# Attention that steps over pairs of heads instead of single heads

## What is computed

```
M1 (mixer of the first block):
  4 memory heads:  p = softmax(q k^T / 8)                       256 queries x 256 memory keys
  6 forgetting heads: p = softmax(q k^T / 8 + c_query - c_key)  causal, c = cumsum(log_f)
  6 gated groups:  out = gelu(u) * (tril(w_s) @ rmsnorm(gelu(v)) + b_s)
MA (sliding window, 16 heads, 2 key/value heads):
  s = q k^T / 8 + bias[t5_bucket(distance)];  window of 128;  softmax with a sink
MB (latent attention, 16 heads, 96-wide q and k):
  s = q k^T / sqrt(96), causal;  q, k normed, 32 of the 96 columns rotated
each: o = p @ v, then o @ w_out added to x
```

## Time and profile before

| | |
|---|---|
| Median of 3 runs | 1393.72 us (1381.62 to 1393.95) |
| Span of the profiled execution | 1392.3 us |
| PE busy | 1329.8 us, 96% of the span, 8874 matmuls |
| DVE busy | 749.8 us, 54% |
| ACT busy | 609.7 us, 44% |
| POOL busy | 116.0 us, 8% |
| Chain that ended last | PE 68% of the span; L244 to L246 20% each, L467 3%, L492 2%, L480 1% |
| Mean granted clock of PE | 0.953 |

### The profile page before, as it was taken

The page is one execution under the profiler, slowest core; times in us unless marked ns, Lnnn a source line. Parts: engine busy times, 40 slices in busy tenths (PEclk is TensorE's granted clock), DMA queues, the critical chain, the costliest instruction groups (busy, mean ns, idle before and its releaser), DMA issues.

```text
span 1392.3 us, 21334 instructions
## 1 busy us (share of the span) xinstructions
PE 1329.8 (96%) x8874; PEld 1200.9 (86%) x8874; DVE 749.8 (54%) x932; ACT 609.7 (44%) x790; POOL 116.0 (8%) x163
## 2 busy tenths in 40 slices
PE   6989989999899999989999999999999889999998
PEld 6885789999799999875889999899999768999997
DVE  4784355555465555564365555555554585555554
ACT  5463244444443344454343344443333586444432
POOL 3440010000210000031000000100000160000000
PEclk9996799999999999985899999999999989999999
DMA  9961035556465555451145555465555402455530
GB/s 312 334 184 42 31 120 184 181 185 209 135 216 182 181 184 192 140 171 35 61 152 182 182 188 191 132 208 190 184 181 172 135 31 65 149 184 191 193 127 31
DMA packets 167091, 220.87 MB, mean 159 GB/s; under 512 B 6014, under 2 KB 148412, under 8 KB 166892
## 3 DMA queue, kind: packets, MB, share of 16 engines
q1 hardware_dynamic: 164572, 212.28, 47.2%
q0 software_dynamic: 2448, 7.58, 1.7%
HBM read 212.47 MB, written 7.37 MB: 158 GB/s over the span
## 4 chain that ended last, share of the span: by engine, by line
PE 68%; DVE 2%; ACT 1%; issue 1%; POOL 0%; POOLq 0%; DVEq 0%; ACTq 0%
PE ps L244 20%; PE ps L245 20%; PE ps L246 20%; PE ps L467 3%; PE ps L492 2%; PE ps L480 1%; PE ps L344 1%; PE ps L493 1%; DVE x L387 1%; ACT w_hi L218 0%; DVE h_lo L365 0%; ACT h_hi L357 0%; POOL rstd L310 0%; PE ps L841 0%; PE ps L842 0%
## 5 line engine op out<-in xcount | busy, mean ns | idle before, releaser
L225 DVE TENSOR_TENSOR w_lo<-raw,w_hi 128x2048 fp32r<-128x2048 f32 x194 | 444.8, 2296 | 291.1 <-ACT w_hi L218 291.0
L218 ACT CAST w_hi<-raw 128x2048 fp32r<-128x2048 f32 x197 | 372.7, 1893 | 340.3 <-PE ps L246 329.9
L244 PE MATMUL ps<-h_hi,w_hi 128*128 128x256 f32 x1744 | 494.6, 284 | 4.0 <-DVE h_lo L365 4.0
L245 PE MATMUL ps<-h_lo,w_hi 128*128 128x256 f32 x1744 | 493.4, 283 | 0.0
L246 PE MATMUL ps<-h_hi,w_lo 128*128 128x256 f32 x1744 | 493.4, 283 | 0.0
L244 PEld LDWEIGHTS ps<-h_hi,w_hi 128*128 128x128 f32 x1744 | 334.4, 192 | 7.2 <-issue 3.0
L245 PEld LDWEIGHTS ps<-h_lo,w_hi 128*128 128x128 f32 x1744 | 334.5, 192 | 2.1
L246 PEld LDWEIGHTS ps<-h_hi,w_lo 128*128 128x128 f32 x1744 | 334.4, 192 | 0.0
L244 PE MATMUL ps<-w_hi,act_hi 128*128 128x512 f32 x480 | 187.6, 391 | 1.3 <-DVE act_lo L914 1.3
L245 PE MATMUL ps<-w_lo,act_hi 128*128 128x512 f32 x480 | 187.4, 390 | 0.0
L246 PE MATMUL ps<-w_hi,act_lo 128*128 128x512 f32 x480 | 186.7, 389 | 0.0
(11 more groups left out here) (218 smaller groups left out, 1079.2 us busy)
## 6 DMA issues: line engine op xcount, KB each, us to landing
raw<-in_ffn_wg SPq DMA_DIRECT2D x44, 1024.0 KB, 5.3
raw<-in_ffn_wu SPq DMA_DIRECT2D x44, 1024.0 KB, 5.3
raw<-in_ffn_wd SPq DMA_DIRECT2D x44, 1024.0 KB, 4.9
raw<-in_w_ff SPq DMA_DIRECT2D x32, 1024.0 KB, 5.3
raw<-in_w_in SPq DMA_DIRECT2D x8, 1024.0 KB, 14.2
raw<-in_a_w_in SPq DMA_DIRECT2D x5, 1024.0 KB, 5.2
canvas<-act POOLq DMA_DIRECT2D x6, 688.0 KB, 11.4
raw<-in_w_out SPq DMA_DIRECT2D x4, 1024.0 KB, 6.7
```

Source lines behind the costliest of these rows:

```text
L218: nc.scalar.copy(w_hi[:, b % RING, 0:n], raw[:, b % RAW, 0:n]).then_inc(hi_ready, 1)
L225: nc.vector.tensor_tensor(w_lo[:, b % RING, 0:n], raw[:, b % RAW, 0:n], w_hi[:, b % RING, 0:n].bitcast(F32), ALU.subtract).then_inc(lo_rea ...
L244: nc.tensor.matmul(to, still[0], moving[0], start=start, stop=False, skip_group_check=True)
L245: nc.tensor.matmul(to, still[0], moving[1], start=False, stop=False, skip_group_check=True)
```

## The change

All three attentions step over pairs of heads. In step `n` PE does the scores of pair `n` with the two heads alternating per query tile (A, B, A, B), then `between`, then the values of pair `n - 3` (also alternating, A, B, A, B), and then the transposes of pair `n - 2`. ACT and DVE do each of their functions for both heads of a pair. `scores_tensor` waits for both maxima of the pair before. The probabilities have four tiles instead of three; those of M1 lie in `scratch`, so that DVE's wait for the canvas stores ahead of M1 is gone. The work in `between` is regrouped to the new steps. No instruction's shape changes.

```diff
-        prob = [arena[:, S_AT:S_AT + 512], arena[:, S_AT + 512:S_AT + 1024], act[:, 2, :]]
+        prob_whole = [scratch[:, 512 * n:512 * n + 512] for n in range(4)]
+        prob_causal = [arena[:, S_AT:S_AT + 384], arena[:, S_AT + 384:S_AT + 768], act[:, 2, 0:384], arena[:, S_AT - 384:S_AT]]
         prob_t = carve(S_AT + 1024, 2, 512)
-        nmx, den, rden, sink_e = (small[:, 160 + 4 * n:164 + 4 * n].rearrange("p (b t) -> p b t", b=2) for n in range(4))
+        nmx, den, rden, sink_e = (small[:, 160 + 8 * n:168 + 8 * n].rearrange("p (b t) -> p b t", b=4) for n in range(4))
...
+            def weights(self, t):
+                at = t * P if self.causal else t * TOK
+                return self.prob[:, at:at + self.keys(t)]
+
+        def scores_tensor(pair):
+            e = pair[0].e
             if e >= 2:
-                nc.tensor.wait_ge(negmax_ready, e - 1)
-            if h.wait_tensor:
-                h.wait_tensor()
+                nc.tensor.wait_ge(negmax_ready, e)
+            for h in pair:
+                if h.wait_tensor:
+                    h.wait_tensor()
             for t in range(TT):
-                n = h.keys(t)
-                to = ps[:, e % 2, t * TOK:t * TOK + n]
-                last = nc.tensor.matmul(to, h.q(t), h.k(n), start=True, stop=h.extra is None, skip_group_check=True)
-                if h.extra:
-                    last = nc.tensor.matmul(to, h.extra[0], h.extra[1](n), start=False, stop=True, skip_group_check=True)
-            last.then_inc(scores_psum, 1)
-
-        def turn_tensor(h):
-            e = h.e
-            nc.tensor.wait_ge(prob_ready, e + 1)
+                n = pair[0].keys(t)
+                for h in pair:
+                    last = nc.tensor.matmul(ps[:, h.e % 2, t * TOK:t * TOK + n], h.q(t), h.k(n), start=True, stop=h.extra is None,
+                                            skip_group_check=True)
+                    if t == TT - 1 and not h.extra:
+                        last.then_inc(scores_psum, 1)
+                for h in pair:
+                    if h.extra:
+                        last = nc.tensor.matmul(ps[:, h.e % 2, t * TOK:t * TOK + n], h.extra[0], h.extra[1](n), start=False, stop=True,
+                                                skip_group_check=True)
+                        if t == TT - 1:
+                            last.then_inc(scores_psum, 1)
+
+        def turn_tensor(pair):
+            e = pair[0].e
             if e >= 2:
-                nc.tensor.wait_ge(turned_ready, e - 1)
+                nc.tensor.wait_ge(turned_ready, e)
+            for h in pair:
+                nc.tensor.wait_ge(prob_ready, h.e + 1)
+                for s in range(TT):
+                    for t in range(s if h.causal else 0, TT):
+                        col = s * TOK + t * P - (s * P if h.causal else 0)
+                        last = nc.tensor.transpose(ps[:, 2 + h.e % 2, col:col + P], h.weights(t)[:, s * P:(s + 1) * P], ident[:, :])
+                last.then_inc(turned_psum, 1)
+
+        def values_tensor(pair):
+            e = pair[0].e
+            n = e // 2
+            nc.tensor.wait_ge(turned_ready, e + 2)
+            if n >= 2:
+                nc.tensor.wait_ge(o_lo_ready, n - 1)
             for s in range(TT):
-                for t in range(s if h.causal else 0, TT):
-                    col = s * TOK + t * P - (s * P if h.causal else 0)
-                    last = nc.tensor.transpose(ps[:, 2 + e % 2, col:col + P],
-                                               prob[e % 3][:, t * TOK + s * P:t * TOK + (s + 1) * P], ident[:, :])
-            last.then_inc(turned_psum, 1)
-
-        def values_tensor(h):
-            e = h.e
-            pair = e // 2
-            nc.tensor.wait_ge(turned_ready, e + 1)
-            if e % 2 == 0 and pair >= 2:
-                nc.tensor.wait_ge(o_lo_ready, pair - 1)
-            q0 = P if h.causal else 0
-            to = ps[h.row:h.row + HD, 4 + pair % 2, :]
-            nc.tensor.matmul(to[:, 0:TOK], h.v(0), prob_t[:, e % 2, 0:TOK], start=True, stop=False, skip_group_check=True)
-            nc.tensor.matmul(to[:, q0:TOK], h.v(1), prob_t[:, e % 2, TOK:2 * TOK - q0], start=False, stop=True,
-                             skip_group_check=True).then_inc(o_psum, 1)
-
-
+                q0 = s * P if pair[0].causal else 0
+                for h in pair:
+                    last = nc.tensor.matmul(ps[h.row:h.row + HD, 4 + n % 2, q0:TOK], h.v(s), prob_t[:, h.e % 2, s * TOK:(s + 1) * TOK - q0],
+                                            start=s == 0, stop=s == TT - 1, skip_group_check=True)
+                    if s == TT - 1:
+                        last.then_inc(o_psum, 1)
+
+        def pairs_of(heads):
+            return [heads[n:n + 2] for n in range(0, len(heads), 2)]
 
         def attention_tensor(heads, between=None):
-            for n in range(len(heads) + 3):
-                if n < len(heads):
-                    scores_tensor(heads[n])
+            pairs = pairs_of(heads)
+            for n in range(len(pairs) + 3):
+                if n < len(pairs):
+                    scores_tensor(pairs[n])
                 if between:
                     between(n)
-                if 2 <= n < len(heads) + 2:
-                    turn_tensor(heads[n - 2])
                 if n >= 3:
-                    values_tensor(heads[n - 3])
+                    values_tensor(pairs[n - 3])
+                if 2 <= n < len(pairs) + 2:
+                    turn_tensor(pairs[n - 2])
...
         def attention_scalar(heads, between=None):
-            for n in range(len(heads) + 4):
+            pairs = pairs_of(heads)
+            for n in range(len(pairs) + 3):
                 if between:
                     between(n)
-                if 2 <= n < len(heads) + 2:
-                    turned_scalar(heads[n - 2])
-                if n < len(heads):
-                    exp_scalar(heads[n])
-                if n >= 4 and n % 2:
-                    out_scalar(heads[n - 4])
+                if n < len(pairs):
+                    for h in pairs[n]:
+                        exp_scalar(h)
+                if n >= 3:
+                    out_scalar(pairs[n - 3][1])
+                if 2 <= n < len(pairs) + 2:
+                    for h in pairs[n - 2]:
+                        turned_scalar(h)
...
         def attention_vector(heads, between=None):
-            for n in range(len(heads) + 5):
+            pairs = pairs_of(heads)
+            for n in range(len(pairs) + 4):
                 if between:
                     between(n)
-                if n < len(heads):
-                    max_vector(heads[n])
-                if 1 <= n <= len(heads):
-                    prob_vector(heads[n - 1])
-                if n >= 6 and n % 2 == 0:
-                    out_vector(heads[n - 5])
+                if n < len(pairs):
+                    for h in pairs[n]:
+                        max_vector(h)
+                if n >= 4:
+                    out_vector(pairs[n - 4][1])
+                if 1 <= n <= len(pairs):
+                    for h in pairs[n - 1]:
+                        prob_vector(h)
...
-                attention_scalar(heads_b, lambda n: turned_qk_scalar(n + 2))
+
+                def next_pair(n):
+                    turned_qk_scalar(2 * n + 2)
+                    turned_qk_scalar(2 * n + 3)
+
+                attention_scalar(heads_b, next_pair)
...
             def gated_split(n):
-                if n == 2:
-
+                if n == 1:
                     vector.wait_ge(mixed_psum, 1)
...
-            vector.wait_ge(canvas_written[0], 32 * CHUNKS)
             attention_vector(heads_m1, gated_split)
...
                 def between_vector(n):
                     if n < TT:
                         whole_keys(n, EARLY_KEYS, BH)
-                    if 2 <= n < 2 + 3 * QUARTERS:
-                        split_quarter(up + 3 + (n - 2) // QUARTERS, (n - 2) % QUARTERS)
+                    if 2 <= n < 8:
+                        for q in (2 * n - 4, 2 * n - 3):
+                            split_quarter(up + 3 + q // QUARTERS, q % QUARTERS)
 
                 attention_vector(heads_b, between_vector)
...
             def gated_turn(n):
-                if n == 1:
+                if n == 0:
                     tensor.wait_ge(v_ready, 1)
                     tensor.wait_ge(ws_t_ready, 3)
...
-                if n == 4:
+                if n == 2:
                     tensor.wait_ge(oa_ready, 1)
...
-                attention_tensor(heads_b, lambda n: turn_qk_tensor(n + 2))
+                def next_pair(n):
+                    turn_qk_tensor(2 * n + 2)
+                    turn_qk_tensor(2 * n + 3)
+
+                attention_tensor(heads_b, next_pair)
```

(14 more changed lines are left out.)

24 lines of the change are left out of this document (10 added, 14 removed).

## The result

| | before | after |
|---|---|---|
| Median | 1381.53 us (20 runs, 1375.79 to 1396.63) | 1388.32 us (20 runs, 1384.04 to 1396.51) |
| Span of the profiled execution | 1392.3 us | 1385.4 us |
| PE busy | 96% | 93% |
| Mean granted clock | 0.953 | 0.959 |

The ratio is 1.0054, with a 95% interval of 1.0035 to 1.0073: 0.5% slower, where 1359 us had been predicted. One thing ahead of all comparisons: the two profiled executions point the other way (-6.9 us). Most runs of the kernel before lie near 1380 us and about one in five near 1395, and the profile that the prediction worked from is one of the latter.

What follows compares the result with a forecast made beforehand. PE alone at 1.2 GHz was taken to bound M1 and MA, with three engines close together in MB. Terms -13 - 22 + 1 = -34 us on 1392.3 gave 1358, stated as 1359 for the median; range 1353 to 1366 (chance 0.66).

Steps and rivals of the forecast that it cites:

- M1: Gated mixer's attention: causal scores start after 112.2, a causal pair's scores cost 5.0 us instead of 7.5; -13 us.
- Overlap: Score and value matmuls of a pair's two heads were taken to overlap fully on the array's two halves.
- MA: Sliding-window attention: about 35 us from first maximum to projection, at about 650 instead of 673.66; taken as -22 us.
- A step is thus 4.7 cold and 3.9 warm: Full pair step in MA: 4.7 us set by PE at low clock, 3.9 by DVE and ACT at full clock.
- The end of the stage: MA's tail, where no scores hide ACT's copies: two steps of 2.2 and a last of 1.3, 5.7 us.
- MB: Latent attention: only values overlap, ACT sets 4.5 us a pair (-2), pipeline three pairs deep (+3); taken as +1 us.
- The clock stays low: Rival: granted clock stays low inside attention; -25 us, 1369. Chance 0.14 for one or both stages.
- Early return: Rival: full clock back early everywhere, M1 -16, MA -24, MB -1, about 1 behind; -42 us, 1351. Chance 0.09.
- Bunching in MB: Rival: nearly full ACT and DVE wait for whole pairs, eight steps lose 1 us each; +8, 1367. Chance 0.07.
- Slower: Rival: each alternation between a pair's score or value matmuls drains the array; +25.5 us, 1419. Chance 0.04.
- steps over 5 us in MB: Sign in the changed profile that would show the forecast wrong through bunching.
- PE waits for DVE and ACT: Sign that the forecast is right: in MA, once the clock rises to 1.00 before its scores end.

Runs made afterwards that it cites:

- before_again: The kernel before, unchanged, profiled a second time and timed against itself: ratio 1.0006, profiled span 1377.1 us.
- run 12: Not a label, but part of "one run 12 us below": one of three runs the prediction had lay 12 us below the others.
- six_tiles: The changed kernel with six probability tiles instead of four in M1 and MA, four kept in MB: 1358.02 us, ratio 0.9780 to the kernel before.
- old_order: The changed kernel, four tiles, with PE's transposes ahead of the values and ACT's copies ahead of its exponentials: 1366.00 us.
- copies_first: The changed kernel, four tiles, with only ACT's copies moved ahead of its exponentials: 1368.05 us.
- six_no_alternation: six_tiles with a pair's score and value products issued one head after the other instead of alternating: 1370.22 us.

## Why the prediction was wrong

**What bounds the kernel.** "PE alone, at 1.2 GHz, sets the pace in M1 and MA" was right for that profile. For M1 the 1.2 GHz do not hold in before_again, which ran the same stretch at 1.00, and its span is that of most runs. The prediction saw the sign of it (one run 12 us below) and then let the sum stand on 1392.3.

**Overlap.** Right. The score matmuls of a pair take 1.65 us cold and 0.93 warm for eight, the values 1.48 and 0.80 from start to start (621.86 to 623.34; 621.08 to 621.88 in six_tiles), against 1.47 and 0.79 in the prediction. The Trainium skill ("TensorEngine Tiling (Array Packing)", Key Properties) says that tiles operate independently of each other; the trace agrees with these numbers.

**MA, the step that failed.** "A step is thus 4.7 cold and 3.9 warm": measured 6.60 at either clock. It adds up the work of each engine and takes the largest sum, as if the engines were free to overlap. Of the waits that cross engines it followed the one for both maxima, and ACT's copy in the tail; the tile wait in `max_vector` it never listed, though four tiles were named in the change, and the exchange of transposes and values, shown in the order of instructions, was given no price. Without this loop the sums come near: old_order, with four tiles, took 42.9 us in MA, and 64 - 22 is 42. The end of the stage, "two steps of 2.2 and a last one of 1.3, 5.7", was mis-sized too, by the order of ACT's calls: the last pair's scores are at 639.07 and the last values at 656.3, with 3.58 us of idle PE for copies behind exponentials. From the first maximum (604.10) to the projection (656.67) it took 52.6 us, not 35.

```profile
604.10 0.34 DVE L571 CUSTOM_DVE_ANT_0 act<-ps,arena,small 128x128 f32<-128x128 f32 x1
...
648.25 1.31 PE L506 MATMUL ps<-arena 128*64 128x256 f32 x8 [3.58 <-ACT arena L542]
...
656.67 0.58 PE L244 MATMUL ps<-w_hi,h_hi 128*128 128x256 f32 x1
```

**M1.** The pair's scores cost 5.0 us as worked out, and causal scores started earlier than the 112.2 laid out, at 109.76, but the end is later: projection at 146.90 where 145 was said, with 3.31 us of the same idle time before the values at 140.21.

```profile
109.76 0.80 PE L474 MATMUL ps<-arena 64*128 64x128 f32 x4 [2.67 <-DVE small L571]
...
140.21 1.55 PE L506 MATMUL ps<-arena 128*64 128x256 f32 x8 [3.31 <-ACT arena L542]
...
146.90 0.39 PE L244 MATMUL ps<-w_hi,h_hi 128*128 128x256 f32 x1
```

So M1 is 10 us shorter than in the profile of the earlier trace rows and 6 longer than in before_again: the term was 3 us off, and what it was measured against was wrong. The two ran at different clocks (0.58 from 118 to 144 us here, 1.00 from 118 to 141.8 in before_again), so how much of the 6 us is the pair steps' own is not shown.

**MB.** "ACT sets 4.5 a pair" gave -2, the deeper pipeline +3. Measured: 5.37 a pair, where the tile wait closes a loop through scores, values and transposes with no engine full (12.22, 12.43 and 13.03 of 16.2 us). Two steps of it (the next scores start at 1150.16, above):

```profile
1139.42 1.58 PE L474 MATMUL ps<-arena 96*128 96x128 f32 x8 [1.32 <-DVE small L571]
...
1144.78 1.58 PE L474 MATMUL ps<-arena 96*128 96x128 f32 x8 [1.30 <-DVE small L571]
```

MB is +8.4 in all, all of it after the last scores start, so the +3 for the end was mis-sized most. The copies behind exponentials are 3.8 us of that end (copies_first); the rest of it is open, as said above.

**Sum and rivals.** Forecast -13 - 22 + 1. Measured against the same profile -10 - 6 + 8.5 = -8, so that M1 missed by 3, MA by 16 and MB by 7.5, together about 26 of the 29 us between 1359 and 1388; against a usual execution +6.3 - 7.2 + 8.4 = +7.5. *The clock stays low*: in part (0.64 in MA, 1.00 at times), but the step did not depend on it. *Early return*: no. *Bunching in MB*: the price of 8 us was right and the cause, ACT and DVE being nearly full, was not. *Slower*: the sign was right and the mechanism wrong; alternation drained nothing. No rival contained a wait on tiles. Of the signs named for the changed profile, "steps over 5 us in MB" came true, and the overlap; "PE waits for DVE and ACT" did too, but in a ring and not because they were full.

## What to carry to other kernels

When the unit of a software pipeline doubles, list every wait that counts in the old unit (tiles, banks, buffers, `e - 3`) and convert it: buffers for three heads in flight become buffers for three pairs, and four tiles for two pairs were fewer than three for three heads. The step's time was here the longest ring of waits through all engines, not the busiest engine's sum; when calls change places inside a step, walk the ring once with durations. Before pricing a change against one profile, compare its span with all the runs. The Trainium skill ("Perfetto Trace Analysis", Optimization Strategy) says that the same gap repeating can mean too few buffers for the next tile; here the 0.99 us ahead of L474 in each full step of MA was such a gap, and in six_tiles, with two tiles more, the scores of the steps shown start without one, and 0.86 us of idle time ahead of the values is left.

## What the runs showed of the hardware

Matmuls of two heads on the two halves of the array overlap without alternating in the program. In six_no_alternation all products of the first head are issued, then all of the second. The eight score records of a pair took 1.66 us at half clock (from 607.11), where the four of a single head took 1.65 before, and 0.93 us at full clock. They begin in twos; the first two, of 0.37 us, lie together in 0.39:

```profile
617.42 0.39 PE L477 MATMUL ps<-arena 64*128 64x128 f32 x2
```

The trace does not name a record's head; that the two are of different heads is read from these lengths. With the extras of M1 between the heads it did not happen, which cost 2.5 us a pair at half clock. And the granted clock differs between executions in the same stretch: with the same instructions in M1 (single heads) it was 0.53, 0.90 and 1.00 from 118 us on, and the stage took 56.4, 44.7 and 39.9 us.
